# One-core diffusion layer step with a routed mixture: the first pair's token gather with the picking matrix stationary

## The chip, the cores and the metric

The kernel runs on one core of one Trainium2 chip. The number that counts is the device time of one execution in microseconds, taken as the median of several runs. Differences below about 0.2% (3.0 us here) can hardly be told from no change.

## The reference, cut to what matters

One trunk layer is computed for 128 context tokens and 256 latent tokens (384 rows of 2048 features, float32): a projection, attention and a short convolution, an output projection, and then a mixture of 16 experts. The part that the change touches is the mixture. Each expert picks the tokens with its largest affinities (16 of the context rows, 32 of the latent rows), runs a gated feed-forward network on them, and adds the weighted result back:

```python
def ec_moe(h, w_router, w_gate, w_up, w_down):
    B, T, D = h.shape
    cap = EC_CAPACITY_FACTOR * T // N_EXPERTS
    logits = jnp.einsum('btd,de->bte', h, w_router).astype(jnp.float32)
    aff = jax.nn.softmax(logits, axis=-1)
    gate, idx = lax.top_k(jnp.swapaxes(aff, 1, 2), cap)
    xs = jax.vmap(lambda hb, ib: hb[ib])(h, idx)
    a = jnp.einsum('becd,edf->becf', xs, w_gate)
    u = jnp.einsum('becd,edf->becf', xs, w_up)
    y = jnp.einsum('becf,efd->becd', jax.nn.silu(a) * u, w_down)
    y = y * gate[..., None].astype(y.dtype)
    ...
```

The gather `xs` is one row selection. The weights of the 16 experts (w_gate and w_up 2048 x 1024, w_down 1024 x 2048 each) are by far the largest data.

## The kernel before

**Pairs of experts.** The mixture runs over 8 pairs of experts. A pair has 64 + 64 = 128 slots (48 of each 64 are in use). TensorE gathers a pair's rows by matrix products with a 0/1 picking matrix: `pick` holds three blocks (`t` = 0, 1, 2, one for each 128 tokens) of 128 tokens x 128 slots. `h2_rows` (tile `mix`) holds the normalised tokens as rows. For the feed-forward network the gathered rows are needed with features on the partitions (`xs`: 16 blocks `k` of 128 features x 128 slots), so each block is made with 128 columns of `h2_rows` as the stationary operand and `pick` as the moving one, added up over the three `t`. Four blocks are one quarter and fill one PSUM bank; DVE then scales and shifts them into `xs` (`first_rows` for the two halves of the first quarter, `xs_out` for the rest) and raises `first_xs` or `xs_ready`.

**The weight ring.** All expert weights stream through `ring`: 8 slots of 2048 KB, or 4 wide slots of 4096 KB (order `WIDE_AT`). In the loop one wide slot holds half of one weight matrix of one expert. In the first pair, whose first expert's gate and up matrices are loaded by `first_load` while the output projection ends, each wide slot `q` holds a quarter of the gate matrix in its lower slot and a quarter of the up matrix in its upper slot. `first_quarters` goes over `q` = 0 to 3: the gate products of the quarter (8 products, each of the two 64-row halves of the array taking 512 columns), a gather of the next quarter, and the up products (8 products).

**What frees the ring.** TensorE's `half_used`, `up_half_used` and `moe_used` tell SyncE that a slot or half of one is free. SyncE's queue waits for each in the written order and issues the next load (`expert_load`, line 552, all in one queue, in order). In the first pair the lower slot is reloaded as one load of 2048 KB (as two quarters of 1024 KB for `q` = 0), and the upper slot as two quarters of 1024 KB, one after each half of the up products. Later loads are 4096 KB each.

**Names in the profile.** All products appear at line 653 (`mm`), all transposes at their own line (one helper's is 663); the pick products of before read `early,mix` (`early` holds `pick`), the expert products `ring,hid` (`hid` holds `xs`). One float32 product is two MATMUL and two LDWEIGHTS instructions in the trace; a transpose is one of each. `y_all`, part of `hid`, holds the pair's results later and nothing of use at this time, but for one row copy that DVE writes into its first 512 columns after the first quarter.

Of the kernel before, what the change touches and what calls it, by code (L numbers as in the profile page):

```python
# [20 lines left out]
P = 128  # L21
D = 2048
KC = D // P
T_CTX, T_LAT = 128, 256
T = T_CTX + T_LAT
NT = T // P
# [16 lines left out]
PW = 2 * ES  # L43
# [5 lines left out]
BLK = 512  # L49
# [68 lines left out]
WIDE = RING // 2  # L118
# [21 lines left out]
WIDE_AT = [4, 0, 2, 6]  # L140
# [6 lines left out]
def build(nc, x_prompt, x_sample, cache_k, cache_v, c, c_ctx, w_ada, b_ada, g_norm1, w_in, g_q, g_k, conv_w,  # L147
          g_attn_out, g_conv_out, w_out, g_norm2, w_router, w_gate, w_up, w_down, consts,
          y_prompt, y_sample, state_k, state_v):
    with ExitStack() as ctx:  # L150
# [3 lines left out]
        def sem(name):  # L154
            return ctx.enter_context(nc.semaphore(name))
# [39 lines left out]
        h2_rows = x_rows  # L195
# [105 lines left out]
        rt_at = moe_at[0]  # L301
        y_all = moe_piece(4 * BANK)
        y_sb = [y_all[:, 0:2 * BANK], y_all[:, 2 * BANK:]]
        give_at = hid_at + 4 * moe_at[0]
        giveT = [moe_piece(T), moe_piece(T)]
        slotP, affP = moe_piece(6 * PAIRS), moe_piece(6 * PAIRS)
# [66 lines left out]
        aff_turned, rank_ready, rank_turned = sem("aff_turned"), sem("rank_ready"), sem("rank_turned")  # L373
        rows_turned, rows_out = sem("rows_turned"), sem("rows_out")
        first_gathered, first_xs = sem("first_gathered"), sem("first_xs")
        first_used, first_landed = sem("first_used"), sem("first_landed")
        pick_ready, gathered, xs_ready, xs_scaled = sem("pick_ready"), sem("gathered"), sem("xs_ready"), sem("xs_scaled")
        give_ready, give_turned, giveT_ready = sem("give_ready"), sem("give_turned"), sem("giveT_ready")
# [57 lines left out]
        def _(sp):  # L436
# [102 lines left out]
            def expert_load(pair, q, sub=None, mats=MATS, quarter=None):  # L539
                what, e = mats[q // 2]  # L540
                part, slot = q % 2, WIDE_AT[q % WIDE]
                if what == "d":
                    src = down_rows[bass.ds(pair * 2 * FF + e * FF + part * BLK, BLK), :].rearrange("(p j) n -> p j n", j=4)
                else:
                    src = (gate_rows if what == "g" else up_rows)[bass.ds(pair * 2 * D + e * D + part * 1024, 1024), :]\
                        .rearrange("(p k) n -> p k n", k=8)
                rows = src.shape[1]
                dst = ring[:, slot:slot + 2, :].rearrange("p s n -> p (s n)").rearrange("p (k n) -> p k n", k=rows)
                lo, hi = (0, rows) if sub is None else (sub * rows // 2, (sub + 1) * rows // 2)
                if quarter is not None:  # L550
                    lo, hi = quarter * rows // 4, (quarter + 1) * rows // 4
                sp.dma_start(dst[:, lo:hi, :], src[:, lo:hi, :]).then_inc(first_landed if quarter == 0 else moe_landed[q % WIDE], 16)
# [29 lines left out]
            for j in range(HALF_FIRST):  # L582
                sp.wait_ge(half_used, j + 1)
                if j == 0:
                    expert_load(0, WIDE, quarter=1)
                else:
                    expert_load(0, j + WIDE, 0)
                sp.wait_ge(up_half_used, j + 1)
                expert_load(0, j + WIDE, quarter=2)
                sp.wait_ge(moe_used, j + 1)  # L590
                expert_load(0, j + WIDE, quarter=3)
            for j in range(HALF_FIRST, PER_PAIR):
                sp.wait_ge(moe_used, j + 1)
                expert_load((j + WIDE) // PER_PAIR, (j + WIDE) % PER_PAIR)
# [56 lines left out]
        def _(pe):  # L651
            def mm(out, lhsT, rhs, start, stop):
                return nc.tensor.matmul(out, lhsT, rhs, start=start, stop=stop, skip_group_check=True)  # L653
# [347 lines left out]
                last = nc.tensor.transpose(bank[2][:, h * RT:(h + 1) * RT], rank[:, h * P:(h + 1) * P], ident[0:RT, 0:RT])  # L1001
            last.then_inc(rank_turned, 1)

            def gather_rows(out, q, kks):
                for kk in kks:
                    k = 4 * q + kk
                    for t in range(NT):
                        last = mm(out[:, kk * PW:(kk + 1) * PW], h2_rows[:, t, k * P:(k + 1) * P],
                                  pick[:, t * PW:(t + 1) * PW], t == 0, t == NT - 1)
                return last  # L1010

            def gather_quarter(q):
                gather_rows(bank[4 + q], q, range(4)).then_inc(gathered, 1)

            def gather(i):

                pe.wait_ge(pick_ready, i + 1)
                for q in range(4):
                    gather_quarter(q)

            def send_chunk(k, b):

# [5 lines left out]
            def up_or_gate(slot, what, e, part, sub, gate_bank, at, kks=range(4)):  # L1028
                for kk in (4 * sub + n for n in kks):
                    k = 8 * part + kk  # L1030
                    for half in range(2):
                        off = kk % 4 * FF + half * BLK
                        last = mm(bank[gate_bank if what == "g" else 1][ES * half:ES * half + ES, :],
                                  xs[:, k, e * ES:(e + 1) * ES], ring[:, slot + at, off:off + BLK], k == 0, k == KC - 1)
                return last
# [59 lines left out]
                    mm(bank[ROW_BANKS[n]][:, :], rows, row_block(y_lo, c), False, True).then_inc(row_sent, 1)  # L1095

            def landed(i, q):
                pe.wait_ge(moe_landed[q % WIDE], 48 * i + 16 * (q // WIDE + 4))

            def turn_give(i, variants=2):  # L1100
                pe.wait_ge(give_ready, i + 1)
# [3 lines left out]
                    last.then_inc(give_turned, 1)  # L1105


            def first_quarters():
                gather_rows(bank[4], 0, range(2)).then_inc(first_gathered, 1)
                gather_rows(bank[1], 0, range(2, 4)).then_inc(gathered, 1)  # L1110

                for q in range(WIDE):
                    pe.wait_ge(moe_landed[q], 32)
                    if q == 0:
                        pe.wait_ge(first_xs, 1)
                        up_or_gate(WIDE_AT[q], "g", 0, 0, 0, 3, 0, range(2)).then_inc(first_used, 1)
                        pe.wait_ge(xs_ready, 1)
                        up_or_gate(WIDE_AT[q], "g", 0, 0, 0, 3, 0, range(2, 4)).then_inc(half_used, 1)
                    else:
                        pe.wait_ge(xs_ready, q + 1)  # L1120
                        up_or_gate(WIDE_AT[q], "g", 0, q // 2, q % 2, 3, 0).then_inc(half_used, 1)
                    if q + 1 < WIDE:
                        gather_quarter(q + 1)
                    up_or_gate(WIDE_AT[q], "u", 0, q // 2, q % 2, 3, 1, range(2)).then_inc(up_half_used, 1)
                    up_or_gate(WIDE_AT[q], "u", 0, q // 2, q % 2, 3, 1, range(2, 4)).then_inc(moe_used, 1)

            def round_of(i, first=False, last_pair=False, turns_res=False):
                mats = LAST_MATS if last_pair else MATS
# [104 lines left out]
        def _(act_e):  # L1233
            a = act_e

            def copy(out, in_):
                return nc.scalar.activation(out, in_, ACT.Copy)  # L1237
# [189 lines left out]
            def rows_copy_out(groups):  # L1427
                for g in groups:
                    a.wait_ge(rows_turned, g + 1)
                    part, half = g // NT // 2, g // NT % 2  # L1430
                    nc.scalar.activation(h2_rows[:, g % NT, part * 1024:(part + 1) * 1024].rearrange("p (a b) -> p a b", a=8)[:, :, 64 * half:64 * half + 64],
                                         bank[ROWS_BANKS[g % len(ROWS_BANKS)]][:, :].rearrange("p (b a) -> p a b", a=8), ACT.Copy,
                                         scale=rstd2[:, g % NT:g % NT + 1]).then_inc(rows_out, 1)
# [2 lines left out]
            nc.scalar.activation(lg, lg, ACT.Exp).then_inc(exp2_done, 1)  # L1436
            a.wait_ge(inv_ready, 1)
            rows_copy_out(range(12))

            def silu(i, e, first):  # L1440
                if first and e == 0:
# [702 lines left out]
```

## Time and profile before

| what | before |
|---|---|
| median of 3 runs | 1519.86 us (1519.55 to 1520.5) |
| the profiled execution | 1520.56 us, span 1518.9 us |
| mixture, from the first gather | 598.5 us to the end of the span |
| PE busy over the span | 1448.1 us (95%) |
| granted TensorE clock, mean | 0.989 of full speed |
| moved by DMA | 572.48 MB, mean 377 GB/s |

A view by windows gives, for each stretch, how long each engine was busy, the granted clock, the busy share of the DMA engines and the rate that they moved. A view in order of time gives for each run of like instructions its start, its duration, and what ended the idle time before it. A view of one source line gives for its DMA issues the time from issue to landing. All times are in microseconds from the span's start.

### The profile page before, as it was taken

Reading aid. Unit: us, or ns where it says so; the run is one execution under the profiler, and the core shown is the slowest. Engines: PE = TensorE matmul, PEld = TensorE weight load, DVE = VectorE, ACT = ScalarE, POOL = GpSimd, SP = SyncE. Lnnn points to the kernel's source line nnn. Section 1 sums busy time; section 2 is a strip of 40 time slices with the busy share of each in tenths; the row PEclk is TensorE's granted clock in tenths of the full one; section 3 lists DMA queues with packets and bytes.
Section 4 is the critical chain, followed back from the end, with each engine's and each line's share of the span. In section 5 each row is a group of like instructions: output and inputs, shape, how many; then the busy total and the mean of one; then the engine's idle time right before and its main releaser. Section 6 shows DMA issues by size and latency. Waiting matters only on the chain.

```text
span 1518.9 us, 18489 instructions
## 1 busy us (share of the span) xinstructions
PE 1448.1 (95%) x7806; PEld 882.3 (58%) x7806; DVE 623.8 (41%) x1033; ACT 255.1 (17%) x358; POOL 26.7 (2%) x58
## 2 busy tenths in 40 slices
PE   6999999999999999999999999999999999899998
PEld 3667799888899997435434335335335335335433
DVE  5454977877799996101301301301301301211313
ACT  4233223333234223000000000000000000000200
POOL 0000000000000000000000000000000000000000
PEclk9999999999999999999999999999999999999999
DMA  9999697777778759999999999999999999999999
GB/s 374 403 395 367 251 332 291 280 259 262 260 274 294 256 172 382 389 433 431 433 431 429 431 433 431 431 432 433 431 431 432 433 430 430 432 433 429 430 423 352
DMA packets 99856, 572.48 MB, mean 377 GB/s; under 512 B 9613, under 2 KB 54613, under 8 KB 76757
## 3 DMA queue, kind: packets, MB, share of 16 engines
q1 hardware_dynamic: 88416, 520.14, 84.0%
q0 software_dynamic: 6912, 50.33, 8.7%
q10 hardware_dynamic: 4468, 1.14, 0.3%
q8 instruction: 45, 0.74, 0.2%
q14 instruction: 15, 0.11, 0.0%
HBM read 565.02 MB, written 6.55 MB: 376 GB/s over the span
## 4 chain that ended last, share of the span: by engine, by line
PE 69%; DMA 23%; DVE 4%; SPq 2%; issue 2%; ACT 1%; DVEq 0%; ACTq 0%
PE psum L653 67%; DMA ring<-in_w_up 18%; DMA ring<-in_w_ada 3%; SPq L563 2%; DMA res<-in_w_ada 1%; DVE res L1664 1%; DMA ring<-in_w_down 1%; DVE w_parts L1537 1%; PE psum L663 0%; DVE ring L1685 0%; PE psum L852 0%; PE psum L1104 0%; SPq L450 0%; PE psum L1074 0%; ACT w_parts L1237 0%
## 5 line engine op out<-in xcount | busy, mean ns | idle before, releaser
L653 PE MATMUL psum<-ring,hid 128*64 128x512 f32 x3024 | 685.6, 601 | 46.4 <-DMA ring<-in_w_up 32.9
L653 PEld LDWEIGHTS psum<-ring,hid 128*64 128x64 f32 x3024 | 243.6, 139 | 464.9 <-issue 416.0
L2000 DVE TENSOR_TENSOR hid<-psum,hid 128x512 f32<-128x512 f32 x16 | 11.1, 692 | 515.0 <-PE psum L653 515.0
L653 PE MATMUL psum<-h_parts,w_parts 128*128 128x384 f32 x1152 | 207.3, 337 | 1.0 <-DVE hid L1713 1.0
L653 PEld LDWEIGHTS psum<-h_parts,w_parts 128*128 128x128 f32 x1152 | 199.8, 188 | 4.8 <-issue 2.5
L1537 DVE TENSOR_TENSOR w_parts<-ring,w_parts 128x2048 fp32r<-128x2048 f32 x52 | 119.0, 2288 | 47.6 <-ACT w_parts L1237 47.3
L1237 ACT ACTIVATE w_parts<-ring 128x2048 fp32r<-128x2048 f32 x52 | 99.6, 1916 | 194.9 <-PE psum L653 163.0
L653 PE MATMUL psum<-w_parts,h_parts 128*128 128x512 f32 x432 | 103.3, 395 | 0.6 <-DVE h_parts L1581 0.6
L653 PE MATMUL psum<-ring,early 128*32 128x512 f32 (+6 forms) x654 | 92.9, 539 | 7.8 <-DMA ring<-in_w_ada 6.7
L653 PEld LDWEIGHTS psum<-w_parts,h_parts 128*128 128x128 f32 x432 | 79.7, 188 | 25.5 <-issue 9.2
L653 PEld LDWEIGHTS psum<-early,mix 128*128 128x128 f32 x768 | 86.6, 192 | 9.0 <-issue 9.0
L653 PE MATMUL psum<-early,mix 128*128 128x128 f32 x768 | 88.6, 276 | 0.8 <-DVE early L1945 0.8
L1453 ACT ACTIVATE hid<-psum 64x1024 f32<-64x1024 f32 x24 | 24.4, 1018 | 330.1 <-PE psum L653 330.0
L653 PE MATMUL psum<-hid 128*128 128x384 f32 (+1 forms) x248 | 77.7, 465 | 0.0
L1664 DVE SCALAR_TENSOR_TENSOR res<-res,early 128x2048 f32<-128x2048 f32 x30 | 69.2, 2347 | 19.1 <-DMA res<-in_w_ada 12.6
L653 PE MATMUL psum<-attn_parts,w_parts 128*128 128x384 f32 x384 | 68.4, 335 | 0.9 <-DVE res L1843 0.9
L653 PE MATMUL psum<-conv_parts,w_parts 128*128 128x384 f32 x384 | 68.4, 335 | 0.2 <-DVE conv_parts L1735 0.2
L653 PEld LDWEIGHTS psum<-attn_parts,w_parts 128*128 128x128 f32 x384 | 66.7, 188 | 1.4 <-DVE res L1843 1.2
L653 PEld LDWEIGHTS psum<-conv_parts,w_parts 128*128 128x128 f32 x384 | 66.5, 188 | 1.5 <-issue 0.8
L653 PEld LDWEIGHTS psum<-hid 128*128 128x128 f32 x248 | 45.7, 190 | 30.4 <-issue 5.7
L1992 DVE SCALAR_TENSOR_TENSOR res<-psum,mod,res 128x128 f32<-128x128 f32 x192 | 63.0, 408 | 0.8
L1685 DVE SCALAR_TENSOR_TENSOR ring<-ring,early 128x2048 f32<-128x2048 f32 x24 | 55.3, 2346 | 0.0
(223 smaller groups left out, 725.7 us busy)
## 6 DMA issues: line engine op xcount, KB each, us to landing
ring<-in_w_up SPq DMA_DIRECT2D x30, 4096.0 KB, 22.7
ring<-in_w_gate SPq DMA_DIRECT2D x28, 4096.0 KB, 29.3
ring<-in_w_down SPq DMA_DIRECT2D x26, 4096.0 KB, 28.7
ring<-in_w_ada POOLq DMA_DIRECT2D x48, 1024.0 KB, 6.8
ring<-in_w_in SPq DMA_DIRECT2D x36, 1024.0 KB, 8.2
ring<-in_w_ada SPq DMA_DIRECT2D x28, 768.0 KB, 15.5
res<-in_w_ada SPq DMA_DIRECT2D x16, 1024.0 KB, 7.2
ring<-in_w_out SPq DMA_DIRECT2D x16, 1024.0 KB, 5.8
```

The source lines that it names most:

```text
L563: sp.dma_start(tail_slot(b, e)[:, 2 * half:2 * half + 2, :], down_pairs(e, 1, half)[:, :, col:col + width])\
L653: return nc.tensor.matmul(out, lhsT, rhs, start=start, stop=stop, skip_group_check=True)
L1237: return nc.scalar.activation(out, in_, ACT.Copy)
L1453: last = nc.scalar.activation(y_sb[half][row:row + ES, :].rearrange("p (b n) -> p b n", b=2), psum[row:row + ES, 2:4, :], ACT.Copy, scale= ...
L1537: tt(w_part(u, 1), raw_unit(u), w_part(u, 0).bitcast(F32), ALU.subtract).then_inc(lo_ready, 1)
L1664: stt(added_up_3[n], chunk_3, cond[:, k, n:n + 1], added_up_3[n], ALU.mult, ALU.add).then_inc(add_done_3, 1)
L1685: stt(sums, rows, cond[:, k, n:n + 1], sums, ALU.mult, ALU.add).then_inc(add_done, 1)
L1992: last = stt(xT[:, k, lo:hi], bank[b][:, lo:hi], mod3[:, 5 * KC + k, n:n + 1], xT[:, k, lo:hi], ALU.mult, ALU.add)
L2000: tt(by_row, bank[1][:, :].rearrange("p (b a) -> p a b", a=4), by_row, ALU.mult).then_inc(act_ready, 1)
```

## The change

For the first pair only, the gather is made the other way round. `pick_rows` makes `pick` stationary and moves the rows of `h2_rows` past it, 256 or 512 columns at a time; the result stands as slots x features in PSUM. ScalarE copies it to `picked` (which is `y_all`), raising `picked_out`, and TensorE turns it with four transposes per quarter (`turn_rows`) into the bank from which DVE took it before. The pick of a quarter stands one step further ahead of its use: quarter 1 is picked ahead of the first gate products, quarters 2 and 3 between the gate and the up products of `q` = 0 and 1, and for `q` = 2 only the transposes are left there. The upper slot is reloaded in two halves only for `q` = 0; for `q` = 1 to 3 it is one load of 2048 KB after all the up products of the slot. The later pairs' `gather` is only written in another form.

```diff
@@ sync @@
-                sp.wait_ge(up_half_used, j + 1)
-                expert_load(0, j + WIDE, quarter=2)
-                sp.wait_ge(moe_used, j + 1)
-                expert_load(0, j + WIDE, quarter=3)
+                if j == 0:
+                    sp.wait_ge(up_half_used, 1)
+                    expert_load(0, WIDE, quarter=2)
+                    sp.wait_ge(moe_used, 1)
+                    expert_load(0, WIDE, quarter=3)
+                else:
+                    sp.wait_ge(moe_used, j + 1)
+                    expert_load(0, j + WIDE, 1)
@@ tensor @@
             def landed(i, q):
-                pe.wait_ge(moe_landed[q % WIDE], 48 * i + 16 * (q // WIDE + 4))
+                pe.wait_ge(moe_landed[q % WIDE], 48 * i + 16 * (q // WIDE + (3 if q % WIDE else 4)))
+            def pick_rows(b, q, lo=0, hi=BLK):
+
+                for t in range(NT):
+                    last = mm(bank[b][:, lo:hi], pick[:, t * PW:(t + 1) * PW], h2_rows[:, t, q * BLK + lo:q * BLK + hi], t == 0, t == NT - 1)
+                return last
+
+            def turn_rows(b, q, kks=range(4)):
+
+                for kk in kks:
+                    last = nc.tensor.transpose(bank[b][:, kk * PW:(kk + 1) * PW], picked[:, q * BLK + kk * P:q * BLK + (kk + 1) * P], ident[:, :])
+                return last
+
             def first_quarters():
-                gather_rows(bank[4], 0, range(2)).then_inc(first_gathered, 1)
-                gather_rows(bank[1], 0, range(2, 4)).then_inc(gathered, 1)
+                pick_rows(5, 0, 0, 2 * P).then_inc(rows_picked, 1)
+                pick_rows(6, 0, 2 * P, 4 * P).then_inc(rows_picked, 1)
+                pe.wait_ge(picked_out, 1)
+                turn_rows(4, 0, range(2)).then_inc(first_gathered, 1)
+                pick_rows(7, 1, 0, 2 * P)
+                pe.wait_ge(picked_out, 2)
+                turn_rows(1, 0, range(2, 4)).then_inc(gathered, 1)
+                pick_rows(7, 1, 2 * P, 4 * P).then_inc(rows_picked, 1)
...
                     if q + 1 < WIDE:
-                        gather_quarter(q + 1)
-                    up_or_gate(WIDE_AT[q], "u", 0, q // 2, q % 2, 3, 1, range(2)).then_inc(up_half_used, 1)
-                    up_or_gate(WIDE_AT[q], "u", 0, q // 2, q % 2, 3, 1, range(2, 4)).then_inc(moe_used, 1)
+                        pe.wait_ge(picked_out, q + 3)
+                        turn_rows(5 + q, q + 1).then_inc(gathered, 1)
+                    if q + 2 < WIDE:
+                        pick_rows(4, q + 2).then_inc(rows_picked, 1)
+                    if q == 0:
+                        up_or_gate(WIDE_AT[q], "u", 0, 0, 0, 3, 1, range(2)).then_inc(up_half_used, 1)
+                        up_or_gate(WIDE_AT[q], "u", 0, 0, 0, 3, 1, range(2, 4)).then_inc(moe_used, 1)
+                    else:
+                        up_or_gate(WIDE_AT[q], "u", 0, q // 2, q % 2, 3, 1).then_inc(moe_used, 1)
@@ scalar @@
             rows_copy_out(range(12))
+            for n, (b, lo, hi) in enumerate(((5, 0, 2 * P), (6, 2 * P, 4 * P), (7, 0, BLK), (4, 0, BLK), (4, 0, BLK))):
+                a.wait_ge(rows_picked, n + 1)
+                at = max(n - 1, 0) * BLK
+                copy(picked[:, at + lo:at + hi], bank[b][:, lo:hi]).then_inc(picked_out, 1)
```

On TensorE, at the start of the first pair, the order before is this (a row is a run of products as written, the shape is that of the output; `early,mix` is the gather, `ring,hid` the gate and up products; a bracket names what the row waits for):

```order
L653 MATMUL psum<-early,mix 128x128 [waits pick_ready,rows_out]
L653 MATMUL psum<-early,mix 128x128 x11
L653 MATMUL psum<-ring,hid 64x512 [waits first_xs,moe_landed0]
L653 MATMUL psum<-ring,hid 64x512 x3
L653 MATMUL psum<-ring,hid 64x512 [waits xs_ready]
L653 MATMUL psum<-ring,hid 64x512 x3
L653 MATMUL psum<-early,mix 128x128 x12
L653 MATMUL psum<-ring,hid 64x512 x8
```

The same place in the changed kernel (`mix,early` are the pick products, `ident,hid` at line 1116 the transposes of `turn_rows`; line 659 is the old line 653):

```order
L659 MATMUL psum<-mix,early 128x256 [waits pick_ready,rows_out]
L659 MATMUL psum<-mix,early 128x256 x5
L1116 MATMUL psum<-ident,hid 128x128 [waits picked_out]
L1116 MATMUL psum<-ident,hid 128x128
L659 MATMUL psum<-mix,early 128x256 x3
L1116 MATMUL psum<-ident,hid 128x128 [waits picked_out]
L1116 MATMUL psum<-ident,hid 128x128
L659 MATMUL psum<-mix,early 128x256 x3
L659 MATMUL psum<-ring,hid 64x512 [waits first_xs,moe_landed0]
L659 MATMUL psum<-ring,hid 64x512 x3
L659 MATMUL psum<-ring,hid 64x512 [waits xs_ready]
L659 MATMUL psum<-ring,hid 64x512 x3
```

Ahead of the first gate products there stood 12 products of 128 columns; now there stand 12 products of 256 columns and 4 transposes. Behind them, between gate and up products, 12 products of 128 columns become 4 transposes and 3 products of 512 columns for `q` = 0 and 1, and 4 transposes alone for `q` = 2.

On SyncE's queue, the ring loads of the first pair before (shapes in float32 elements of each partition: 2048 is 1024 KB in all, 4096 is 2048 KB):

```order
L552 DMA ring<-in_w_gate 128x2048 [waits first_used]
L552 DMA ring<-in_w_gate 128x2048 [waits half_used]
L552 DMA ring<-in_w_gate 128x2048 [waits up_half_used]
L552 DMA ring<-in_w_gate 128x2048 [waits moe_used]
L552 DMA ring<-in_w_gate 128x4096 [waits half_used]
L552 DMA ring<-in_w_gate 128x2048 [waits up_half_used]
L552 DMA ring<-in_w_gate 128x2048 [waits moe_used]
L552 DMA ring<-in_w_down 128x4096 [waits half_used]
L552 DMA ring<-in_w_down 128x2048 [waits up_half_used]
L552 DMA ring<-in_w_down 128x2048 [waits moe_used]
```

and in the changed kernel:

```order
L554 DMA ring<-in_w_gate 128x2048 [waits first_used]
L554 DMA ring<-in_w_gate 128x2048 [waits half_used]
L554 DMA ring<-in_w_gate 128x2048 [waits up_half_used]
L554 DMA ring<-in_w_gate 128x2048 [waits moe_used]
L554 DMA ring<-in_w_gate 128x4096 [waits half_used]
L554 DMA ring<-in_w_gate 128x4096 [waits moe_used]
L554 DMA ring<-in_w_down 128x4096 [waits half_used]
L554 DMA ring<-in_w_down 128x4096 [waits moe_used]
```

From the second slot on, two loads of 1024 KB behind two signals have become one of 2048 KB behind the later signal; 13 loads are now 10.

## Rows read from the trace of the kernel before

**Rows 1.** By windows: first pair, a pair in the loop, near the end.

```profile
core 0: us, PE busy (x) PEld busy (x) DVE busy (x) ACT busy (x) POOL busy (x), PEclk, DMA share, GB/s
598.00:694.00 96.00, 94.37 (x530) 47.95 (x530) 16.38 (x47) 4.88 (x7) 0.00 (x0) 1.00 1.00 410
950.00:1060.00 110.00, 103.56 (x498) 47.16 (x496) 20.21 (x55) 6.13 (x8) 0.00 (x0) 0.97 1.00 432
1400.00:1480.00 80.00, 78.28 (x381) 30.80 (x379) 17.16 (x28) 11.51 (x20) 0.00 (x0) 1.00 1.00 426
```

**Rows 2.** Line 552, all loads issued from 645 to 1450 us.

```profile
DMA to landing us min/median/max: 13.9/26.0/33.2
```

**Rows 3.** Chain of work that ended last, in order of time.

```profile
1343.20 27.59 DMA ring<-in_w_up
```

**Rows 4.** In order of time, TensorE in the first pair.

```profile
598.48 2.75 PEld L653 LDWEIGHTS psum<-early,mix 128*128 128x128 f32 x24 [0.92 <-issue]
598.51 2.92 PE L653 MATMUL psum<-early,mix 128*128 128x128 f32 x24 [0.81 <-DVE early L1945]
601.36 3.65 PE L653 MATMUL psum<-ring,hid 128*64 128x512 f32 x16
604.94 2.94 PE L653 MATMUL psum<-early,mix 128*128 128x128 f32 x24
607.82 7.09 PE L653 MATMUL psum<-ring,hid 128*64 128x512 f32 x32
638.86 13.95 PE L653 MATMUL psum<-ring,hid 128*64 128x512 f32 x64
```

**Rows 5.** In order of time: transposes, 384-column products, DVE and ACT steps.

```profile
588.54 2.35 PE L663 MATMUL psum<-ident,res 128*128 128x128 f32 x20
735.89 10.59 PE L653 MATMUL psum<-hid 128*128 128x384 f32 x32
600.20 0.49 DVE L1984 TENSOR_TENSOR hid<-psum,perm_raw 128x64 f32<-128x64 f32 x2 [0.97 <-PE psum L653]
600.72 0.49 DVE L1984 TENSOR_TENSOR hid<-hid,perm_raw 128x64 f32<-128x64 f32 x2
638.64 0.87 ACT L1237 ACTIVATE hid<-psum 128x384 f32<-128x384 f32 x2 [3.30 <-PE psum L1104]
```

**Rows 6.** In order of time, SyncE's queue, loads of the first pair.

```profile
603.34 18.40 SPq L552 DMA_DIRECT2D ring<-in_w_gate  x7
624.84 13.65 SPq L552 DMA_DIRECT2D ring<-in_w_down  x6
645.99 7.19 SPq L552 DMA_DIRECT2D ring<-in_w_up  x2
```

**Rows 7.** Single loads: issue, and time to landing (lines 511 and 552).

```profile
L511 SPq DMA_DIRECT2D ring<-in_w_gate x1: 341/341/341, 572.2 to 572.2; - x1
DMA to landing us min/median/max: 7.4/7.4/7.4
...
L511 SPq DMA_DIRECT2D ring<-in_w_gate x1: 328/328/328, 597.2 to 597.2; - x1
DMA to landing us min/median/max: 9.0/9.0/9.0
...
L552 SPq DMA_DIRECT2D ring<-in_w_gate x1: 328/328/328, 609.8 to 609.8; - x1
DMA to landing us min/median/max: 5.2/5.2/5.2
...
L552 SPq DMA_DIRECT2D ring<-in_w_gate x1: 328/328/328, 621.4 to 621.4; - x1
DMA to landing us min/median/max: 7.9/7.9/7.9
...
L552 SPq DMA_DIRECT2D ring<-in_w_down x1: 328/328/328, 638.2 to 638.2; - x1
DMA to landing us min/median/max: 11.3/11.3/11.3
```

More of the change, by code:

```diff
@@ L303, in build @@
         y_sb = [y_all[:, 0:2 * BANK], y_all[:, 2 * BANK:]]
+        picked = y_all
         give_at = hid_at + 4 * moe_at[0]
@@ L375, in build @@
         first_gathered, first_xs = sem("first_gathered"), sem("first_xs")
+        rows_picked, picked_out = sem("rows_picked"), sem("picked_out")
         first_used, first_landed = sem("first_used"), sem("first_landed")
@@ L1002, in _ @@
             last.then_inc(rank_turned, 1)
[L1004 to L1013, printed above, removed]
             def gather(i):
                 pe.wait_ge(pick_ready, i + 1)
-                for q in range(4):
-                    gather_quarter(q)
+                for k in range(KC):
+                    for t in range(NT):
+                        last = mm(bank[4 + k // 4][:, k % 4 * PW:(k % 4 + 1) * PW], h2_rows[:, t, k * P:(k + 1) * P],
+                                  pick[:, t * PW:(t + 1) * PW], t == 0, t == NT - 1)
+                    if k % 4 == 3:
+                        last.then_inc(gathered, 1)
             def send_chunk(k, b):
@@ L1105, in turn_give @@
                     last.then_inc(give_turned, 1)
-            def first_quarters():
-                gather_rows(bank[4], 0, range(2)).then_inc(first_gathered, 1)
-                gather_rows(bank[1], 0, range(2, 4)).then_inc(gathered, 1)
+            def pick_rows(b, q, lo=0, hi=BLK):
+                for t in range(NT):
+                    last = mm(bank[b][:, lo:hi], pick[:, t * PW:(t + 1) * PW], h2_rows[:, t, q * BLK + lo:q * BLK + hi], t == 0, t == NT - 1)
[4 more added lines that the diff above has]
+                return last
+            def first_quarters():
+                pick_rows(5, 0, 0, 2 * P).then_inc(rows_picked, 1)
[6 more added lines that the diff above has]
+                pick_rows(7, 1, 2 * P, 4 * P).then_inc(rows_picked, 1)
                 for q in range(WIDE):
```

## The prediction

> **What bounds the kernel now.** I began with the windows over the mixture. In the loop the DMA engines are busy all the time and move 432 GB/s, and near the end 426 with a busy share of 1.00 again; in the first pair it is 410 [rows 1]. So the whole mixture is bound by the stream of weights, and the first pair is the one stretch that moves less than the loop does. 96 us at 410 instead of 432 GB/s are 96 x (1 - 410/432) = 4.9 us of stream lost: no more than that can be won there. Next I asked whether a loss in the first pair could be caught up later. Every load issued from 645 to 1450 us took 13.9 us or more to land [rows 2]; a 4096 KB load with nothing ahead of it needs about 12.3 (below). So from there on the queue always holds work, and the chain of waits ends PE's last wait on the loop's loads at 1370.8 us on a load of 27.6 us [rows 3]. The stream is then rigid: if it is d late at 650 us, the kernel ends d late, and what PE gains or loses is without effect unless it moves an issue into an empty queue. The first pair is where it does: its loads are issued from 603.34 to 638.16 us, each when PE frees a slot [rows 6].
>
> **How PE and the queue go together.** The expert products cost (13.95 - 7.09)/32 = 0.2144 us for an instruction [rows 4], and the two 64-row halves of the array run side by side, so that 512 columns take 0.4288 us. The first gate products begin at 601.36; eight instructions later it is 603.08, and the load behind `first_used` is issued at 603.34 [rows 4, 6]: an issue follows PE's nominal end by 0.26. A change between the two kinds of product costs 0.15 on the way to the gather (601.36 + 3.43 = 604.79, it starts at 604.94) and 0.13 on the way back (604.94 + 2.75 = 607.69, then 607.82) [rows 4]. With this the issues of before are 603.34, 605.05 (`q` 0 lower), 609.79, 611.51 (upper), 614.94, 619.69, 621.40 (`q` 1), 624.84, 629.58, 631.29 (`q` 2), 634.73, 636.4, 638.16 (`q` 3).
>
> **The gather's new price.** Before, a quarter is 24 instructions in 2.75 us, 0.1146 each, set by the weight loads [rows 4]. Now it is three products of 512 columns, so six instructions, and four transposes. A transpose costs 2.35/20 = 0.117 [rows 5]; I take 0.115, so 0.46 for four. A wide product on the whole array isn't in the trace with 512 columns. Nearest is the one with 384: 10.59/32 = 0.331 [rows 5], which gives 0.441 for 512; the expert products give 0.429. I take 0.43: 2.58 for a quarter, 1.29 for half of one. The sum is 3.04 against 2.75, so PE pays 0.29 more for each quarter, 1.2 over the four. Nothing becomes cheaper, since the same columns times blocks stream through: the weight loads that bounded the old form cost hardly more than its columns.
>
> The Trainium skill (TensorE: Matmul & The Clock Gate, Back-to-back issue gap) speaks for the change more strongly: it gives a sustained spacing of 81 ns for a product with 128 columns and 131 ns for one with 512. By that ratio the three wide products would take 0.40 of the twelve narrow ones, 1.1 us and not 2.6; the row with 384 columns speaks against it.
>
> **The new order on PE.** It starts at 598.51 as before. Picks of the first two halves end at 599.80 and 601.09. ScalarE copies the first meanwhile: a 384-column copy takes 0.435 and starts some 0.25 after PE [rows 5], so 256 columns are out by about 600.5; no wait. Two transposes to 601.32, `first_gathered`. DVE's four steps took 600.20 to 601.21 [rows 5], 0.31 behind PE's end; now 601.63 to 602.64. PE meanwhile picks half of quarter 1 (602.61), turns (602.84) and picks the other half (604.13), so that `first_xs` is no wait; with the hand-over the gate products start at 604.28 instead of 601.36, 2.92 late. Of this 0.29 is the gather's price, 2.58 is quarter 1's pick done ahead of time. What is behind it in PE's queue is the very signal for which SyncE's queue waits.
>
> The new issues: 606.26, 607.97; then 0.15 + 3.04 + 0.13 for turn and pick: 613.0, 614.7; 618.15; again turn and pick, then all the up products, 624.9; 628.33; only transposes (0.74 in all), 632.5; 635.93; 639.36. Late against before: 2.9 (twice), 3.2 (three times), 3.5 for the whole upper slot of `q` 1 (its first half 5.2), 3.5, then 1.2 to the end of the pair.
>
> **What the stream makes of it.** Single loads tell the rule [rows 7]: with nothing ahead 1024 KB land 5.2 us after issue and 2048 KB 7.4 (so 4096 KB some 12.3); otherwise they land one after another, at best 2.43 us per 1024 KB (432 GB/s), in this stretch (621.4 + 7.9 = 629.3 to 638.2 + 11.3 = 649.5, eight of 1024 KB) 2.53. `first_load`'s last one lands at 597.2 + 9.0 = 606.2 in both. From there on the new issues give landings at 611.5, 614.0, 618.2, 620.6, 625.6, 632.3, 637.3, 642.1, 647 and 651.8 (2.43) or 652.6 (2.53). Before it is 649.5. Two places make the loss: the dry queue behind 606.2, and the load at 624.9, which comes 7.4 before its landing while the one ahead of it landed at 625.6. Were it still in halves, 623.2 and 624.9, both would be there at 630.9 and not at 632.3: 1.4 of the loss is the merging at `q` 1. At `q` 2 and 3 merging costs nothing, as the queue then holds a load of 4.9 us.
>
> The first 4096 KB load landed at 645.99 + 13.9 = 659.9. Its issue is 1.2 late now and doesn't matter. The stream brings it at 651.8 + 9.7 = 661.5 at the earliest, 1.6 late. The same rule puts before's last small load at 646.9 to 647.9, 1.6 to 2.6 early against the trace; if the changed kernel has the same small losses, it is 654.3 + 9.7 = 664.0, 4.1 late. I take the middle, **+2.9 us** (1.6 to 4.1), since the unexplained losses lie at the loads that find an empty queue, and there are fewer of these now but drier ones. SyncE's three fewer issues are worth nothing, for it waits on PE all the time. In the later pairs the same instructions stand in the same order.
>
> **The rivals.** *The delay is absorbed*: the losses of before's many 1024 KB loads go with the merging, and the stream is 0 to 1.2 late. For it: 2.53 against 2.43 over the last eight. Against it: 8 x 0.1 is all there is. 1520.5 us, 16 in 100. *The pick is cheap*: the wide product takes 0.2144 for 512 columns, if what the expert rows show isn't two halves side by side. Then a quarter costs 1.29 + 0.46 = 1.75, the gate products start at 601.8, the issues run 0.4 late, then 0.6, 1.6 and 3.9 early, the queue is never dry after 627.3 and the last small load lands at 647.2: 2.3 us less, 1517.6. This one ends on the faster side; it decides from 0.38 per 512-column instruction downwards, where a quarter costs what it did. For it: the 384-column row may be paced by DVE, which empties its banks. Against it: 0.331 is within 4% of what 0.429 scales to. 8 in 100. *A stall in the hand-over*: ScalarE's first copy must be done 1.29 after its pick. If a table load or a late start takes another 0.7 (the estimate is 0.6 to 0.7 for start and copy), PE stands, and `first_used` and all behind it move by as much; three more such hand-overs follow while the queue is dry. At 0.4 to 0.8 each that is 1.2 to 3.5 on top, 1525.2 us. For it: four waits that weren't there. Against it: all but the first have 1.3 us or more of other products between copy and turn. 15 in 100. 1 in 100 is for what I don't see.
>
> **How the numbers follow.** The profiled execution took 1520.56 us, 0.7 above the median of the runs; 1520.56 + 2.9 = 1523.5 there, so **1522.8** as a median. The forecast itself (1.6 to 4.1 us more) has 60 in 100. 0.2%, about what a measurement of this kernel can tell, is 3.0 us: 27 of the 60 lie above, 33 below. Slower: 27 + 15 = 42. Same: 33 + 16 + 4 (half of the cheap pick) = 53. Faster: 5. The range leaves out the cheap pick and the long stalls: 1519.8 to 1525.0.
>
> **What would show it.** Right: 512-column pick instructions 0.43 apart; the first `ring,hid` run near 604.3 and the first load of the ring near 606.3; at 624.9 a load of 2048 KB that lands 7.4 later; a window from 603 to 626 below before's rate; the first 4096 KB load landing 2 to 4 us late, and every loop load late by the same amount. Wrong: pick instructions at 0.22; PE waiting for ACT ahead of a transpose; a ring that at 650 us is where it was; or a shift there that doesn't reach the end, because somewhere in the loop the queue runs dry.

## The result and the profile after

The changed kernel takes 1522.13 us (median of 22 runs, 1521.79 to 1525.67), the kernel before beside it 1519.88 (22 runs, 1519.04 to 1520.71). The ratio is 1.0019, 95% interval 1.0013 to 1.0025: 2.0 to 3.8 us more, 2.9 at the middle. The means of the two sets differ by 2.9 us as well, the medians only by 2.3: five of the changed kernel's 22 runs took more than 1524 us. The profiled execution took 1521.98 us with a span of 1520.3.

By windows, the changed kernel, the three stretches of [rows 1]:

```profile
598.00:694.00 96.00, 94.88 (x484) 44.43 (x482) 15.19 (x43) 7.94 (x12) 0.00 (x0) 1.00 0.95 396
950.00:1060.00 110.00, 103.50 (x506) 47.38 (x504) 20.22 (x55) 6.14 (x8) 0.00 (x0) 0.98 1.00 431
1400.00:1480.00 80.00, 79.71 (x395) 32.49 (x395) 16.54 (x28) 13.58 (x24) 0.00 (x0) 1.00 1.00 426
```

The last two are as they were (431 against 432 GB/s, 426 against 426). Only the first pair moves less, 396 against 410 GB/s, with a DMA share of 0.95 against 1.00. 96 x 14/432 = 3.1 us of stream are missing there. Most of it is missing early. From 603 to 626 us, the changed kernel:

```profile
603.00:626.00 23.00, 23.00 (x97) 8.24 (x98) 3.69 (x11) 3.07 (x4) 0.00 (x0) 1.00 0.80 295
```

and the kernel before:

```profile
603.00:626.00 23.00, 23.00 (x133) 11.65 (x130) 3.31 (x9) 0.00 (x0) 0.00 (x0) 1.00 0.94 350
```

TensorE (with one row of its weight loads) and ScalarE in order of time, the changed kernel, to be laid beside [rows 4]:

```profile
597.25 2.46 PEld L659 LDWEIGHTS psum<-mix,early 128*128 128x128 f32 x12 [0.92 <-issue]
597.28 2.83 PE L659 MATMUL psum<-mix,early 128*128 128x256 f32 x12 [0.81 <-DVE early L1972]
598.85 0.38 ACT L1260 ACTIVATE hid<-psum 128x256 f32<-128x256 f32 x1 [2.60 <-PE psum L659]
599.94 0.38 PE L1116 MATMUL psum<-ident,hid 128*128 128x128 f32 x2
...
603.07 3.65 PE L659 MATMUL psum<-ring,hid 128*64 128x512 f32 x16
...
606.65 0.66 PE L1116 MATMUL psum<-ident,hid 128*128 128x128 f32 x4
607.14 2.74 PE L659 MATMUL psum<-mix,early 128*128 128x512 f32 x6
609.82 7.09 PE L659 MATMUL psum<-ring,hid 128*64 128x512 f32 x32
...
638.06 0.87 PE L1103 MATMUL psum<-ident,early 128*128 128x128 f32 x6
```

The mixture begins at 597.28 here and at 598.51 in [rows 4], so times are compared from the first gather's start. The gate products begin 5.79 behind it against 2.85 (601.36 - 598.51): 2.94 late, where 2.92 was forecast. Six wide pick instructions take (609.82 - 607.14 - 0.13)/6 = 0.425 us each against 0.43. ScalarE's copy ends at 599.23, 0.7 ahead of the transposes, and no transpose waits for it. PE is through with the four slots at 638.06, 40.78 behind the start; before it was at 638.05, 39.54 behind its start: 1.24 late against 1.2. The row of the kernel before:

```profile
638.05 0.87 PE L1104 MATMUL psum<-ident,early 128*128 128x128 f32 x6
```

Single loads of the changed kernel (lines 513 and 554), beside [rows 7]: the last of the first loads, the first ring load, the lower and the merged upper load of q 1, and the first load of 4096 KB.

```profile
L513 SPq DMA_DIRECT2D ring<-in_w_gate x1: 328/328/328, 596.0 to 596.0; - x1
DMA to landing us min/median/max: 8.8/8.8/8.8
...
L554 SPq DMA_DIRECT2D ring<-in_w_gate x1: 327/327/327, 605.0 to 605.0; - x1
DMA to landing us min/median/max: 4.8/4.8/4.8
...
L554 SPq DMA_DIRECT2D ring<-in_w_gate x1: 328/328/328, 616.9 to 616.9; - x1
DMA to landing us min/median/max: 9.3/9.3/9.3
...
L554 SPq DMA_DIRECT2D ring<-in_w_gate x1: 328/328/328, 623.7 to 623.7; - x1
DMA to landing us min/median/max: 9.7/9.7/9.7
...
L554 SPq DMA_DIRECT2D ring<-in_w_up x1: 328/328/328, 646.0 to 646.0; - x1
DMA to landing us min/median/max: 16.6/16.6/16.6
```

The first ring load goes out at 605.04, 0.2 behind the landing at 604.8 of the load ahead of it. A window on the 3 us around it shows what that does to the stream; the same 3 us of the kernel before stand below it in a fence of their own (share of the DMA engines and GB/s in the last two columns):

```profile
603.00:606.00 3.00, 3.00 (x15) 1.06 (x16) 0.84 (x3) 0.60 (x1) 0.00 (x0) 1.00 0.08 22
```

```profile
603.00:606.00 3.00, 3.00 (x19) 1.49 (x16) 0.46 (x1) 0.00 (x0) 0.00 (x0) 1.00 0.78 257
```

The queue is empty. The window finds the kernel before 1.2 us earlier in its mixture; its second profile, whose mixture began at 597.14, moves 328 GB/s in the same window.

The merged load of q 1, issued at 623.7, lands 9.7 later and not 7.4. But the queue wasn't empty for it: the lower load of q 1, issued at 616.9, lands only at 616.9 + 9.3 = 626.2, so that the merged load has 2.6 us to wait and lands 7.1 behind the one ahead. The late one is the lower load. The kernel before, too, took 9.3 us for it:

```profile
L552 SPq DMA_DIRECT2D ring<-in_w_gate x1: 328/328/328, 614.9 to 614.9; - x1
DMA to landing us min/median/max: 9.3/9.3/9.3
```

The first 4096 KB load lands at 646.0 + 16.6 = 662.6, 65.3 behind the mixture's start; before, 645.99 + 13.9 = 659.9 [rows 2, 6] is 61.4 behind it. That is 3.9 late, inside the 1.6 to 4.1 of the forecast and above its middle.

Of all loads after it the quickest still takes 16.6 us (issued 645 to 1450), more than the 12.3 that are estimated for 4096 KB with nothing ahead, so the queue doesn't run dry again:

```profile
DMA to landing us min/median/max: 16.6/27.1/31.7
```

The two spans differ by 1.4 us and not by 3.9, for two reasons. The kernel before began its mixture 1.2 us later in this profile, and between its last two long waits on the loop's loads it lost what the changed kernel didn't: its wait of 27.59 us ended at 1370.79 [rows 3], 59.8 us behind the end of the one ahead of it, and here it is 58.5. The row of the chain:

```profile
1345.84 26.22 DMA ring<-in_w_up
```

That both are drift from one execution to the next is shown by the second profiles of the two kernels: the kernel before began at 597.14 and took 58.9 us between the same two waits, and the changed kernel, which took 857.7 us from the landing at 662.6 to the end of its span, took 860.1 in its second profile (before: 859.0 and 859.4).

### The profile page after: what moved, and what is told of

It is laid out like the page before. It is cut to its first block, busy times and chain, and to the rows that moved or that the text cites. A ratio compares the mean times of both kernels' runs of the same rounds, so it can differ in the third digit from the quotient of the medians.

```text
span 1520.3 us, 18408 instructions
## 1 busy us (share of the span) xinstructions
PE 1445.0 (95%) x7762; PEld 878.8 (58%) x7762; DVE 624.1 (41%) x1033; ACT 257.8 (17%) x363; POOL 26.8 (2%) x58
## 4 chain that ended last, share of the span: by engine, by line
PE 72%; DMA 21%; DVE 3%; SPq 2%; issue 1%; ACT 1%; DVEq 0%; ACTq 0%
PE psum L659 69%; DMA ring<-in_w_up 20%; SPq L565 1%; DMA ring<-in_w_ada 1%; DMA ring<-in_w_down 1%; SPq L452 1%; DVE w_parts L1564 1%; PE psum L669 0%; DVE ring L1712 0%; PE psum L858 0%; PE psum L1103 0%; PE psum L1073 0%; ACT w_parts L1260 0%; DVE mix L1849 0%; PE psum L821 0%
## 5 line engine op out<-in xcount | busy, mean ns | idle before, releaser
L659 PEld LDWEIGHTS psum<-early,mix 128*128 128x128 f32 x672 | 75.6, 192 | 5.7 <-issue 5.7
L659 PE MATMUL psum<-early,mix 128*128 128x128 f32 x672 | 76.9, 276 | 0.0
```

## The experiments

Three theories stood against mine. Mine, the **stream theory**: the ring loads of the first pair go out late, into an empty queue, and the end is as late as the stream. The **PE-price theory**: the new form costs PE 1.2 us, and that goes to the end. The **merge theory**: the larger loads of the upper slots cost it all. The **order theory**: only that the gathers stand a step ahead costs. The measure from the trace, the landing of the first 4096 KB load behind the start of the first gather, is called "the landing" below: 61.4 before, 65.3 changed. The kernels ran in three groups, each beside the kernel before on the same chip.

**Halves restored (`e1_halves`, `e1_again`), merging alone (`e2_merge`).** The edit of the first, made to the changed kernel (PE's side likewise), and in reverse to the kernel before:

```diff
-                    sp.wait_ge(moe_used, j + 1)
-                    expert_load(0, j + WIDE, 1)
+                    sp.wait_ge(up_half_used, j + 1)
+                    expert_load(0, j + WIDE, quarter=2)
+                    sp.wait_ge(moe_used, j + 1)
+                    expert_load(0, j + WIDE, quarter=3)
```

> The changed kernel with the upper slots of all four q reloaded in halves again. Stream theory (the weight stream runs dry when PE frees slots late; the end moves with the landings): the 1024 KB load at q 1 goes out 1.7 us sooner into an empty queue, so the first 4096 KB load lands 1.4 us sooner than in the changed kernel (there 65.3 us behind the first pick's start, here about 63.9), and the time is 1.0 to 1.6 us above before. Merge theory (the larger loads cost it all): 0 above before. PE-price theory (PE's 1.2 us of extra work in the pair passes to the end whatever the loads do): still 2.3 to 2.9 above before.

> The kernel before with only the upper slots of q 1 to 3 loaded whole. Stream theory: at q 1 the merged load would be issued at 621.4 while the load ahead lands at 624.2, so the merging is nearly hidden: 0 to 0.7 us above before. Merge theory: 2.3 to 2.9 above. PE-price theory: 0.

Measured: halves restored 1523.58 us, ratio 1.0026 (1.0016 to 1.0036), landing 64.2. Merging alone 1521.56 us, ratio 1.0011 (1.0002 to 1.0020), landing 61.9. At the landing both look as expected: the restored halves take 1.1 off (1.4 forecast), the merging alone adds 0.5. The times went otherwise: the first was forecast 1.0 to 1.6 us above before and came out 3.9 above by the medians (2.4 to 5.5 by the ratio's interval), no quicker than the changed kernel, and the second was 1.7 us slower than before, of which its landing explains 0.5. The merge theory falls, for it wanted the first at before's time; the PE-price theory, which wanted it 2.3 to 2.9 above, is the one that this run alone would favour. How much the merging costs at the end was left open, and the first was measured again, beside the changed kernel:

> The changed kernel again, beside the next two on one chip, since the halves restored at q 1 to 3 had brought the first 4096 KB load 1.1 us sooner but not the end. All theories: as before, 2.3 to 2.9 us above the kernel before, the first 4096 KB load landing 65.3 us behind the first pick's start.

> The changed kernel with all upper slots in halves, again. If its 3.9 us above before were the drift of the stream from run to run, it is now below the changed kernel by about 1 us on the same chip (stream theory). If the halves do harm later on, it is again 1 us above it.

Measured on one chip: changed kernel 1523.98 us, 1.0023 (1.0013 to 1.0033), landing 64.7; with halves 1523.1 us, 1.0021 (1.0012 to 1.0030), landing 64.5. The halves save 0.9 us by the medians and 0.3 by the ratios, less than the intervals can tell. Over both profiles of each, the landings are 65.0 and 64.35. That is 0.65 us between them at the landing, not the 1.4 that I had put on the merging, and not even this is shown to be the merging's. The lower load of q 1 is issued 19.7 us behind the start in all four profiles, ahead of the first place where the two programs differ, and yet it lands 29.0 and 30.6 behind the start in the changed kernel and 27.8 and 29.6 with the halves: the kernels with halves were 1.2 and 1.0 us ahead before any merged load. At the end the merging's share isn't shown either.

The lower and the merged load of q 1 in the second profile of the changed kernel, whose mixture began at 597.78:

```profile
L554 SPq DMA_DIRECT2D ring<-in_w_gate x1: 327/327/327, 617.4 to 617.4; - x1
DMA to landing us min/median/max: 10.9/10.9/10.9
...
L554 SPq DMA_DIRECT2D ring<-in_w_gate x1: 328/328/328, 624.2 to 624.2; - x1
DMA to landing us min/median/max: 9.0/9.0/9.0
```

Here the lower load lands at 628.3, 4.1 us after the merged one was issued, and the merged one 4.9 behind it, no longer than in a full queue.

**The order alone, in the old form (`e4_ahead`).** To the kernel before:

```diff
                 gather_rows(bank[1], 0, range(2, 4)).then_inc(gathered, 1)
+                gather_quarter(1)
...
-                    if q + 1 < WIDE:
-                        gather_quarter(q + 1)
+                    if q + 2 < WIDE:
+                        gather_quarter(q + 2)
```

> The kernel before with its own narrow gather, in the order of the changed one: quarter 1 gathered ahead of the first gate products, quarter q + 2 between gate and up products of q = 0 and 1, nothing there for q = 2; all upper slots in halves. PE has 0.3 us less to do than before (one pair of hand-overs less). Stream theory: 1.2 to 2.8 us above before, the ring loads of q 0 and 1 being 2.7 us late. PE-price theory: 0.3 below before. Merge theory: 0.

Measured: 1522.12 us, ratio 1.0016 (1.0007 to 1.0025), landing 64.0, so 2.6 late, 2.4 us slower by the medians. Its PE, in order of time:

```profile
597.28 5.60 PE L653 MATMUL psum<-early,mix 128*128 128x128 f32 x48 [0.81 <-DVE early L1946]
602.81 3.65 PE L653 MATMUL psum<-ring,hid 128*64 128x512 f32 x16
...
636.48 0.87 PE L1104 MATMUL psum<-ident,early 128*128 128x128 f32 x6
```

PE ends the four slots at 39.20, 0.3 sooner than before, and the kernel is slower all the same. There is no wide product, no copy by ScalarE and no merged load in it. The PE-price theory wanted it 0.3 faster.

**Lateness alone (`e8_late`).** To the kernel before, ahead of the first gate products:

```diff
+                for _ in range(12):
+                    mm(bank[7][:, 0:P], ident[:, :], ident[:, :], True, True)
```

> The kernel before with 24 instructions of identity products (2.75 us, their result isn't used) ahead of the first gate products, so that all ring loads of the pair go out 2.75 us late and nothing else differs. Stream theory: the empty stretches all move, the first 4096 KB load lands 2.5 to 3 us late, and the end is as late. If late loads of the pair were caught up later, 0 to 1. Order and form theories have nothing here: 0.

Measured: 1522.91 us, ratio 1.0018 (1.0009 to 1.0027); landing 647.4 + 14.2 = 661.6, so 64.4, 3.0 late. It shows the same empty stretch. Its single load and its window:

```profile
L552 SPq DMA_DIRECT2D ring<-in_w_up x1: 328/328/328, 647.4 to 647.4; - x1
DMA to landing us min/median/max: 14.2/14.2/14.2
```

```profile
603.00:606.00 3.00, 3.00 (x16) 0.86 (x12) 0.00 (x0) 0.00 (x0) 0.00 (x0) 1.00 0.29 52
```

2.75 us of work for nothing, placed so that it only makes the ring loads late, cost 2.8 us by the medians (1.4 to 4.1 by the interval). What PE loses here isn't caught up. The order theory, which has nothing here, doesn't account for it.

**PE's price alone (`e5_tail_price`).** To the kernel before, behind the last up products of the four slots:

```diff
                     first_quarters()
+                    for _ in range(5):
+                        mm(bank[0][:, 0:P], ident[:, :], ident[:, :], True, True)
```

> The kernel before with 1.15 us of products of the identity added on PE behind the last up products of the first four slots (ten instructions, their result isn't used), so that PE has the new form's extra work and nothing else of the change. The next ring load (the first of 4096 KB) goes out 1.15 us late, when the queue still holds work. Stream theory: 0 to 0.5 us above before. PE-price theory: 1.15 above.

Measured: 1520.06 us, ratio 1.0000 (0.9991 to 1.0009), landing 645.8 + 13.1 = 658.9, so 61.8 (start 597.12).

```profile
L552 SPq DMA_DIRECT2D ring<-in_w_up x1: 327/327/327, 645.8 to 645.8; - x1
DMA to landing us min/median/max: 13.1/13.1/13.1
```

The load waits 13.1 instead of 14.0 in the second profile of before (below), because it is issued 1.15 later into a queue that still holds work. Ahead of the gates 2.75 us cost 3.0 of the landing; here 1.15 us cost 0.3, and two profiles of one kernel differ by 0.1 (before) to 0.6 (changed). The medians are 0.15 us apart. The interval alone, 1.4 us either way, would not exclude the 1.15 of the PE-price theory; it falls by this and by `e4_ahead` together, where PE had less to do and the kernel was 1.1 to 3.8 us slower.

**The first signal alone (`e3_late_pick`).** The second half of quarter 1's pick in the changed kernel moved behind the first half of the gate products.

```diff
-                pick_rows(7, 1, 2 * P, 4 * P).then_inc(rows_picked, 1)
...
                         up_or_gate(WIDE_AT[q], "g", 0, 0, 0, 3, 0, range(2)).then_inc(first_used, 1)
+                        pick_rows(7, 1, 2 * P, 4 * P).then_inc(rows_picked, 1)
```

> The changed kernel with the second half of quarter 1's pick moved behind the first half of the first gate products; PE's work is the same. The first ring load goes out about 1.4 us sooner, all later ones when they did. Stream theory in its fine form: the queue is dry again before the third load (issued 4 to 5 us later), so what is won at the first two is lost there: 0 to 0.5 us below the changed kernel. Rival (the dry stretch behind the last of the first loads is what costs): 1.3 us below the changed kernel. PE-price theory: as the changed kernel.

Measured: 1522.73 us, ratio 1.0023 (1.0013 to 1.0033), landing 64.5, against 65.3 and 64.7 in the two profiles of the changed kernel. Sending one load sooner, when the next ones are as late as before, gives between 0.2 and 0.8 at the landing and nothing that the times can tell. The rival's 1.3 us isn't there. That what is won at the first loads is lost again at the third fits, but between two profiles of one kernel that lie 0.6 apart it isn't shown.

**The form at the old places (`e6_form_only`).** To the changed kernel; the pick of quarter 1 ahead of the gate products is taken out as well, and the upper slots are in halves as in `e1_halves` (neither is shown):

```diff
-                    if q + 2 < WIDE:
-                        pick_rows(4, q + 2).then_inc(rows_picked, 1)
+                        pick_rows((7, 4, 4)[q], q + 1).then_inc(rows_picked, 1)
...
+                    if q + 1 < WIDE:
+                        pe.wait_ge(picked_out, q + 3)
+                        turn_rows(5 + q, q + 1).then_inc(gathered, 1)
```

> The new form (wide picks, copies by ScalarE, transposes) at the old places: only quarter 0 is picked ahead of the first gate products, quarter q + 1 between gate and up products of q, its transposes between the two halves of the up products; all upper slots in halves. The gate products start 1.3 us late (waiting for first_xs), and 0.3 are added at each q, so that PE ends the four slots 2.2 us late. Stream theory: the first 4096 KB load lands 0.5 to 2 us late, less than with the picks a step ahead (2.6 to 3.1), and the time is as much above before. Order theory (only the gathers' being a step ahead costs): 0. PE-price theory: 2.2 above.

Measured: 1523.83 us, ratio 1.0026 (1.0017 to 1.0036), landing 65.6, so 4.1 late. The order theory falls, for it wanted this kernel at before's time. My numbers for it were too low: PE was through with the four slots 3.4 us late and not 2.2, for I had left out the two hand-overs more at each q, and the first wait is plain in the rows:

```profile
600.46 0.44 PE L1112 MATMUL psum<-ident,hid 128*128 128x128 f32 x2 [0.26 <-ACT hid L1251]
601.47 3.65 PE L655 MATMUL psum<-ring,hid 128*64 128x512 f32 x16 [0.57 <-DVE hid L2002]
```

Here the first 4096 KB load is issued at 648.0, 1.7 us ahead of the landing of the one ahead of it, and lands 13.0 behind that one instead of 9.7: its issue binds it, and PE's price no longer lies behind the queue. The pick's being a step ahead is thus not what is wrong with the change; without it the new form is no better. It moved the place of the loss: late loads at q 0 and 1 in the one, late loads everywhere in the other.

**Before again (`b0_again`), and a finer release (`e7_fine`).**

> The kernel before itself, for a second profile of it, since its first profile began the mixture 1.1 to 1.5 us later than those of five other kernels whose program is the same up to there. All theories: no difference in time. The first 4096 KB load should land 61 to 62 us behind the first gather's start, and the mixture should begin near 597.3 us; if the first profile was typical, 598.5.

> The kernel before, narrow gather, with each gather moved between the two halves of the up products (so that the first half of the upper slot is freed 2.9 us sooner) and the lower slot of q 1 reloaded in two quarters, the first 1.7 us sooner. PE's work is the same. Stream theory: less of the queue's dry time, 0 to 1.5 us below before; the most that the first pair can give is the 1.6 us by which the first 4096 KB load lands later than its issue alone would make it. PE-price and order theory: 0.

The edit of the second, on PE (the signal after half of the gate products of q 1, and SyncE's two quarters behind it, aren't shown):

```diff
-                    if q + 1 < WIDE:
-                        gather_quarter(q + 1)
                     up_or_gate(WIDE_AT[q], "u", 0, q // 2, q % 2, 3, 1, range(2)).then_inc(up_half_used, 1)
+                    if q + 1 < WIDE:
+                        gather_quarter(q + 1)
```

Measured: before again 1519.71 us, ratio 0.9999 (0.9990 to 1.0008), mixture from 597.14, landing 644.6 + 14.0 = 658.6, so 61.5. Its rows:

```profile
597.14 2.92 PE L653 MATMUL psum<-early,mix 128*128 128x128 f32 x24 [0.80 <-DVE early L1945]
```

```profile
L552 SPq DMA_DIRECT2D ring<-in_w_up x1: 328/328/328, 644.6 to 644.6; - x1
DMA to landing us min/median/max: 14.0/14.0/14.0
```

So the first profile of before, the one behind all the rows ahead of the prediction, began its mixture 1.4 us later than usual; the distance from there to the landing is the same (61.4 and 61.5). The finer release: 1519.67 us, ratio 0.9999 (0.9990 to 1.0008), landing 61.4, so the gain, expected at 0 to 1.5 us, can't be told from none. It brings the middle loads forward, but the last ones of the pair go out when they did and bind again. I found no version quicker than before.

## Why the prediction was right, and where it was off

**The bound.** Right: the loop's rate stayed, the first pair's fell from 410 to 396 GB/s, and in `e8_late` a delay of the ring loads by 2.75 us came out at the end whole (2.8 by the medians).

**The gather's price on PE.** Right: 0.425 us for the wide instruction against 0.43, and 1.24 us more in all against 1.2. The "cheap pick" rival is out. The ratio that the Trainium skill (TensorE: Matmul & The Clock Gate, Back-to-back issue gap) gives for 512 and 128 columns, 131 to 81 or 1.6, doesn't hold for these float32 products: 0.425 to 0.1146 is 3.7.

**The hand-over to ScalarE.** Right for the changed kernel: its copy came 0.7 ahead of its use. That rival is real in another place: in `e6_form_only` PE waits 0.26 for ScalarE and 0.57 for DVE.

**The new issues.** Right: the gate products 2.94 late against 2.92. The main term of the loss, late loads at q 0 and 1, is shown by `e4_ahead` (landing 2.6 late with the order alone) and `e8_late`. PE's 1.2 us alone were put at nothing, being hidden by the queue; `e5_tail_price` shows 0.3 at the landing and no time that can be told from none. The three parts, 2.6 for the order, 0.65 between whole and half loads and 0.3 for PE, add up to 3.55 (the middle one isn't shown to be the merging's), against 3.9 and 3.2 in the two profiles of the changed kernel.

**The lower load of q 1** is where the rule for the stream was mis-sized. The prediction took 7.4 us for 2048 KB from a load that had nothing ahead of it, put its issue at 618.15 and its landing at 625.6, 27.1 behind the start. It was issued when forecast, but landed 29.0 and 30.6 behind the start in the two profiles of the changed kernel, 1.9 and 3.5 late, for it took 9.3 and 10.9 us. When it was issued the load of 1024 KB ahead of it still had 3.0 and 3.9 us to go, and it came 6.4 and 7.0 behind that one, where loads of its size in a full queue come 4.9 apart. From the merged load on the stream ran as forecast, 4.9 us for each 2048 KB, and the last small load landed 55.6 and 55.0 behind the start where the rule had 53.3 to 54.1. The row of the kernel before at 614.9, with 9.3 us, had shown the same before the change.

**The small losses.** In before the last small load came 1.6 to 2.6 us behind the rule; in the changed kernel it is 1.5 to 2.3 in the first profile and 0.9 to 1.7 in the second. The step that took them as fewer there, and so chose the middle, +2.9 us, was wrong: they are nearly all there, and the landing was 3.9 and 3.2 late. One reading behind the rule was also off: the 1024 KB load issued at 609.8, which took 5.2 us "with nothing ahead", had one ahead that landed at 611.7. With nothing ahead the changed kernel's load at 605.0 took 4.8.

**The merging at q 1**, "1.4 of the loss", isn't borne out. It rested on the merged load's finding an empty queue, 0.7 us before the landing ahead of it. As the lower load was late, it had 2.6 and 4.1 us to wait, so that its 9.7 and 9.0 us are no price of a load in an empty queue. The traces give 1.1 and 0.2 at the landing in the two pairs of profiles and 0.5 in `e2_merge`. Between two profiles of before, or of kernels with the same order up to there, the lower load alone differs by 0.8 to 2.7 us.

**The time** came out at 1522.13 against 1522.8, the ratio at 1.0019, just what +2.9 gives. The landing would have given 3.2 to 3.9; from the landing to the end the 13 profiles took between 857.7 and 860.3 us, so the runs drift by about as much as the effect itself. That the time hit the middle of the range is in part luck.

**What stays open** is the merging's cost at the end, where `e2_merge` has 1.7 us (0.3 to 3.0) against 0.5 at its landing, and `e1_again` is 0.3 to 0.9 below the changed kernel. Open, too, is why the lower load of q 1 takes so long.

## What to carry to other kernels

When a kernel is bound by a stream of loads through a ring, look for the few places where the queue is empty or nearly so. There the time of the engine that frees the slots can pass whole to the kernel (2.75 us cost 2.8 here), and behind a full queue it may cost nothing that can be measured (1.15 us cost 0.15). Work that prepares a later step costs when it stands ahead of the first instruction that frees a slot, even if the engine does no more in all. To price a load, look also at what was still under way when it was issued. In the same way, a form with fewer and wider products wasn't cheaper here, for the narrow ones already took about the time of their columns, and the transposes came on top.

## What the runs showed that I had not expected

A load that is issued while one or two small loads are still under way took longer than its size and the earlier rows would give. The lower load of q 1 (2048 KB) is such a one in all kernels that load it whole: in 12 profiles it came 4.9 to 7.0 us behind the load ahead of it, in 9 of them 5.6 or more, while in the changed kernel loads of that size later in the pair come 4.9 apart. Its landing also varies where nothing in the program does: 27.8 to 30.6 behind the start in the four profiles with one and the same order up to there. I have no run that gives the cause.

The saturated stream isn't equally fast in every execution. `e2_merge` was 0.5 late at the landing and 1.8 when PE waited for the stream at 787 us, both counted from the mixture's start against the first profile of before (0.4 and 1.2 against the second). The part ahead of the mixture varied as well: the mixture began between 597.03 and 598.51 us over 13 profiles. For differences of 1 us in 1520 the landing in the trace tells more than the time of a run, and neither suffices alone. The changed kernel's times also spread wider than before's beside it (1521.79 to 1525.67 against 1519.04 to 1520.71).
